# Dilated attention on one core: the high and low key halves of the strided branches as one moving operand, their logit halves added by VectorE

## The chip, the core and the metric

The kernel runs on one core of a Trainium2 chip. The metric is the device time of one launch in microseconds (us), from three timed runs and one profiled execution. TensorE ran at a granted clock of 0.999 of full speed over the profiled execution, which is the upper of its two levels, 2.4 GHz.

## What is computed

Two transformer blocks on 512 tokens of width 1024, all in float32. Only one stage of the second block is touched, the dilated attention: 8 heads of width 64, in three groups of keys (window 128 with dilation 1, window 512 with dilation 4, window 2048 with dilation 16), each with a bias per distance. The groups are merged by their row maxima and sums.

```python
s = jnp.einsum('bnqrhc,bnkrhc->bnrhqk', qb, kc) * (HEAD_DIM ** -0.5)
...
logits = jnp.where(valid[None, :, None, None], s + bias[None, None, None], NEG_INF)
m = jnp.max(logits, axis=-1)
p = jnp.exp(logits - m[..., None])
den = jnp.sum(p, axis=-1)
num = jnp.einsum('bnrhqk,bnkrhc->bnqrhc', p, vc)
```

## The kernel before

**Split operands.** TensorE multiplies in a rounded float32 format, so each operand is held as a high part (the rounded value) and a low part (the rest). A product is three matmuls into one PSUM sum: high times high, low times high, high times low. `mm3` (L514 to L518) does that for the dense layers, whose weights stream from memory in units of 128 x 1024: ScalarE rounds a unit (`whi`, L1125), VectorE makes the rest (`wlo`, L1421), TensorE multiplies it in 24 matmuls of 512 columns.

**The attention stage.** The 36 units of the query, key and value projection (`dil`) are multiplied one after the other. TensorE's stream is written by hand: after every second tile of a unit (6 matmuls) comes a "tick", and `attend(tick)` puts a piece of attention work there, by the tables `LOGITS_AT`, `TURN_AT`, `SUMS_AT`, `V_TURN_AT` and others. VectorE and ScalarE walk the same ticks in the same order. Attention is cut into 32 steps: four pairs of heads, each with four strided steps (`part` 0, the two dilated groups side by side, n = 0 to 3 of every eight) and four window steps (`part` 1). The two heads of a pair lie in partitions 0 to 63 and 64 to 127 of `dqk`, so that each logits matmul uses 64 rows. `dqk[rows, o, j, :]` holds for key group o the query high, query low, key high and key low (j = 0 to 3), 512 tokens each.

**One step n.** TensorE multiplies the logits (L972) into banks 2 and 3, one bank for each head. VectorE adds the bias into `dl` (L1957) and takes the negated row maxima (L1960). ScalarE takes the exponentials of both heads with their sums (L1388, `dp`). Two or three ticks after the logits TensorE transposes the probabilities (L984, "turned"), after a wait for the exponentials (`s_dac`). ScalarE and VectorE split them (L1378, L1944), and TensorE multiplies them with the values (L1001 and L1002, "sums"), after waits for the split probabilities and, in the first step of each branch, for the split values (`s_dvs`). The values are transposed by L1015 and split by VectorE (L1440 and L1441 into `dvt`). Before the logits of step n TensorE waits until VectorE has added the bias of step n - 1 (`s_dad`), because all steps use the same two banks.

**A strided step.** Keys are every fourth token: the moving operand is `dqk[r, o, b, t::4]`, 128 columns that lie 16 bytes apart. For each of two groups o and three products there is one matmul for each head, 12 in all.

In a strided step VectorE meets other duties in its fixed order: the projection rows that come out of the banks (L1887, L1470), the rest of the next weight unit (L1421), the value split (L1440, L1441), and the output addition (L1970).

Of the kernel before, what the change touches and what calls it, by code (L numbers as in the profile page):

```python
# [22 lines left out]
ALU = mybir.AluOpType  # L23
# [3 lines left out]
P = 128  # L27
T = 512
# [173 lines left out]
def build(nc, wst, xT, prm, cst, wup, wsT, bs, rb, onehot, fdram, out):  # L202
    es = ExitStack()
    with es:
        def sb(name, shape, dt=F32, st=es):
            return st.enter_context(nc.sbuf_tensor(name, shape, dt))

        def sem(name):
            return es.enter_context(nc.semaphore(name))
# [5 lines left out]
        h = sb("h", [P, KD, T])  # L215
# [18 lines left out]
        def bank(b, n=1):  # L234
            return PS[:, b * T:(b + n) * T]
# [58 lines left out]
        with ExitStack() as m:  # L294
# [3 lines left out]
            dqk = sb("dqk", [P, 3, 4, T], F32R, m)  # L298
# [4 lines left out]
            dl = sb("dl", [P, 2, 2, 256], F32, m)  # L303
# [48 lines left out]
        def bias_of(p):  # L352

            return (bias_a if p < 2 else bias_b)[:, 2 * (p % 2):2 * (p % 2) + 2, :]
# [139 lines left out]
        s_dtr = sem("dilated_transposed")  # L494
        s_dpv = sem("dilated_values_multiplied")
        s_dad = sem("dilated_bias_added")
        s_dlg = sem("dilated_logits_done")
        s_dco = sem("dilated_outputs_half_copied")
        s_dac = sem("dilated_exp_done")
# [14 lines left out]
        def mm3(pe, o, w, x, first, done, **kw):  # L514

            pe.matmul(o, w[0], x[0], start=first, stop=False, **kw)  # L516
            pe.matmul(o, w[1], x[0], start=False, stop=False, **kw)  # L517
            return pe.matmul(o, w[0], x[1], start=False, stop=done, **kw)  # L518
# [35 lines left out]
        def _(pe):  # L554
# [89 lines left out]
            for k, j in [(k, j) for k in range(KD) for j in range(2)]:  # L644
# [4 lines left out]
                ins = mm3(pe, bank(j), w_tile(j, k), x_tile(k), k == 0, k == KD - 1)  # L649
# [59 lines left out]
            for what, p in GLA_PLAN:  # L709
                if (what, p) in GLA_UNITS:  # L710
                    n = GLA_UNITS.index((what, p))
# [141 lines left out]
            for f in range(2):  # L853
                for j in range(4):
                    u = U0["cgv"] + 4 * f + j
                    unit_ready(u)
                    for kk in range(2):
                        k = 2 * j + kk
                        if f == 0:
                            pe.wait_ge(s_x, X0["ffout"] + k + 1)  # L860
                        for t in range(NT):
                            if f and k == 0 and t == 0:
                                pe.wait_ge(s_free, A0["cgu"])
                            if f and k == 0 and t >= 2:
                                pe.wait_ge(s_cac, t - 1)
                            c = slice(t * P, (t + 1) * P)
                            ins = mm3(pe, bank(CG_BANKS[f][t]), (xhi[:, k, c], xlo[:, k, c]),
                                      (whi[:, u % SLOTS, kk * T:(kk + 1) * T], wlo[:, u % SLOTS, kk * T:(kk + 1) * T]),
                                      k == 0, k == KD - 1)
# [7 lines left out]
            for n in range(2):  # L877
                ins = over_partitions(bank(4 + n), wsr[:, 0, 4 * n:4 * n + 4, :], wsr[:, 1, 4 * n:4 * n + 4, :])
# [77 lines left out]
            def logits(n):  # L956
                p, part, t = step_of(n)
                if n % 4 == 0:
                    pe.wait_ge(s_dqk, 6 * p + (6 if part else 4))
                if n:  # L960
                    pe.wait_ge(s_dad, n)
                rows = [slice(0, 64), slice(64, 128)]
                if part:
                    c = slice(T - (t + 1) * P, T - t * P)
                    k0 = (t - 1) * P if t else 0
                    blocks = [(2, c, slice(k0, (t + 1) * P), slice(0 if t else P, 2 * P))]
                else:
                    blocks = [(o, slice((3 - t) * P, (4 - t) * P), slice(t, T, 4), slice(o * P, (o + 1) * P)) for o in range(2)]
                for i, (o, q, k, c) in enumerate(blocks):
                    for a, b in ((0, 2), (1, 2), (0, 3)):  # L970
                        for x, r in enumerate(rows):
                            ins = pe.matmul(bank(2 + x)[:, c], dqk[r, o, a, q], dqk[r, o, b, k], start=i == 0 and (a, b) == (0, 2),  # L972
                                            stop=b == 3, skip_group_check=True)
                ins.then_inc(s_dlo, 1)
# [101 lines left out]
            for m in LAST_PARTS:  # L1076
                if m < 4:
                    acc_wait(A0["dilout"] + 4 + m)
                ins = mm3(pe, part_bank(m), w_tile(u % SLOTS, m), out_pair(3), m < 4, True)
# [332 lines left out]
        def _(dve):  # L1412
# [97 lines left out]
            for what, p in DVE_GLA_PLAN:  # L1510
                E = 11 * p
                if (what, p) in GLA_UNITS:
                    n = GLA_UNITS.index((what, p))
# [32 lines left out]
                elif what == "states":  # L1546

                    for x in range(2):
                        r = slice(64 * x, 64 * x + 64)
# [204 lines left out]
            for t in range(NT):  # L1754
                ins = dve.bn_aggr(mv[:, t, 0:2], st6[:, t, :, :].rearrange("p a b -> p (a b)"))
# [4 lines left out]
            for g in range(KD):  # L1760
                ins = dve.scalar_tensor_tensor(bsb[:, g, :], bank(4 + g // 4)[:, g % 4 * P:(g % 4 + 1) * P], par[:, C_LNB + g:C_LNB + g + 1],
                                               bsb[:, g, :], ALU.mult, ALU.add)
# [184 lines left out]
            def logits_masked(n):  # L1947

                p, part, t = step_of(n)
                o, tt = (oA, t) if part else (oB, 3 - t)  # L1950
                c0 = first_col(n)
                b0 = 0 if part else 256
                z = bank(2, 2).rearrange("p (x c) -> p x c", x=2)
                dve.wait_ge(s_dlo, n + 1)
                if n >= 2:
                    dve.wait_ge(s_dac, n - 1)
                dve.tensor_tensor(dl[:, n % 2, :, c0:], z[:, :, c0:256], bias_of(p)[:, :, b0 + c0:b0 + 256],  # L1957
                                  ALU.add).then_inc(s_dad, 1)
                dve.wait_ge(s_dad, n + 1)
                dve.tensor_reduce(o[:, tt, p, NMAX:ROW], dl[:, n % 2, :, c0:], AX, ALU.max, negate=True).then_inc(s_dlg, 1)  # L1960

# [27 lines left out]
            for tick in range(LAST_TICK):  # L1989
                k, q = tick // TICKS, tick % TICKS  # L1990
# [247 lines left out]
```

## Time and profile before

| | us |
|---|---|
| median of three runs | 1901.11 |
| lowest and highest | 1900.96, 1902.65 |
| the profiled execution, whole | 1901.1 |
| its span in the trace | 1899.4 |
| TensorE busy in the span | 1887.4 (99%) |
| VectorE busy | 1136.0 (60%) |
| ScalarE busy | 622.3 (33%) |

The profiled execution's time lies at the median of the runs; 1.7 us of it lie outside the traced span. The span is the time from the first to the last record. An engine's busy time is the union of its instructions. TensorE has two rows of records: PE for matmuls and PEld for the loads of the stationary operand, which run beside matmuls. The attention stage lies between 1276 and 1526 us of the span.

### The profile page before, as it was taken

To read this page: it belongs to the slowest core of one execution; us is meant where nothing else is said; L and a number is where in the kernel's file an instruction comes from. 1 tells how busy PE (TensorE), PEld (TensorE's weight loads), DVE (VectorE), ACT (ScalarE), POOL (GpSimd) and SP (SyncE) were. 2 spreads that over 40 slices of the span, in tenths; PEclk is the share of its full clock that TensorE was granted. 3 is DMA by queue.
4 is the path that set the end of the run, shared out by engine and by line. 5 is a ranking of instruction groups with operands and counts; after the bars stand their busy time and mean duration, and the time that the engine had idled before them with its cause. 6 is when DMAs were issued, how large, how long until landed. Compare 5 with 4: busy or idle time off the path is not lost.

```text
span 1899.4 us, 24463 instructions
## 1 busy us (share of the span) xinstructions
PE 1887.4 (99%) x9088; PEld 1560.0 (82%) x9088; DVE 1136.0 (60%) x1470; ACT 622.3 (33%) x846; POOL 140.9 (7%) x141
## 2 busy tenths in 40 slices
PE   9999999999999999999999999999999999999998
PEld 6888888888888888888888888888888888888887
DVE  7787777776666434675642354366766786325533
ACT  6313243343333233334322222323333353212221
POOL 0011002300000011002000000100110120000000
PEclk9999999999999999999999999999999999999999
DMA  4222222332233333222332443322222223332332
GB/s 166 67 78 90 78 67 78 100 100 93 95 99 99 96 114 124 79 85 84 111 95 95 116 119 99 98 89 73 79 72 73 62 69 121 100 100 89 99 100 67
DMA packets 54653, 176.48 MB, mean 93 GB/s; under 512 B 5875, under 2 KB 12291, under 8 KB 54572
## 3 DMA queue, kind: packets, MB, share of 16 engines
q1 hardware_dynamic: 49296, 170.82, 28.2%
q10 hardware_dynamic: 4764, 3.41, 0.8%
q0 software_dynamic: 512, 1.08, 0.2%
q8 instruction: 60, 0.98, 0.2%
q14 instruction: 21, 0.17, 0.0%
HBM read 172.09 MB, written 2.13 MB: 92 GB/s over the span
## 4 chain that ended last, share of the span: by engine, by line
PE 97%; DVE 2%; DMA 0%; issue 0%; ACT 0%; SPq 0%; DVEq 0%
PE ps L516 31%; PE ps L518 30%; PE ps L517 30%; PE ps L972 1%; PE ps L524 1%; PE ps L1001 1%; PE ps L984 1%; PE ps L1002 1%; PE ps L767 0%; DVE wlo L1421 0%; DVE yr L1440 0%; PE ps L1015 0%; DMA raw<-wst 0%; DVE h L2029 0%; DVE gate_a L1678 0%; DVE yr L1441 0%
## 5 line engine op out<-in xcount | busy, mean ns | idle before, releaser
L516 PE MATMUL ps<-xhi,whi 128*128 128x512 f32 x1576 | 624.4, 396 | 0.9 <-DVE xlo L1427 0.6
L518 PE MATMUL ps<-xlo,whi 128*128 128x512 f32 x1576 | 614.5, 390 | 0.0
L517 PE MATMUL ps<-xhi,wlo 128*128 128x512 f32 x1576 | 613.9, 390 | 0.0
L1421 DVE TENSOR_TENSOR wlo<-raw,whi 128x1024 fp32r<-128x1024 f32 x317 | 407.7, 1286 | 220.6 <-ACT whi L1125 220.3
L1125 ACT ACTIVATE whi<-raw 128x1024 fp32r<-128x1024 f32 x317 | 334.1, 1054 | 586.7 <-PE ps L518 530.9
L516 PEld LDWEIGHTS ps<-xhi,whi 128*128 128x128 f32 x1576 | 296.1, 188 | 67.4 <-DVE wlo L1421 3.7
L518 PEld LDWEIGHTS ps<-xlo,whi 128*128 128x128 f32 x1576 | 295.8, 188 | 63.1
L517 PEld LDWEIGHTS ps<-xhi,wlo 128*128 128x128 f32 x1576 | 296.2, 188 | 58.2 <-issue 0.2
L516 PE MATMUL ps<-mh,whi 128*128 128x512 f32 (+1 forms) x528 | 202.3, 383 | 0.0
L517 PE MATMUL ps<-mh,wlo 128*128 128x512 f32 (+1 forms) x528 | 202.0, 383 | 0.0
L518 PE MATMUL ps<-mh,whi 128*128 128x512 f32 (+1 forms) x528 | 202.0, 383 | 0.0
L516 PEld LDWEIGHTS ps<-mh,whi 128*128 128x128 f32 x528 | 99.2, 188 | 19.7 <-issue 0.4
L517 PEld LDWEIGHTS ps<-mh,wlo 128*128 128x128 f32 x528 | 99.3, 188 | 19.4
L518 PEld LDWEIGHTS ps<-mh,whi 128*128 128x128 f32 x528 | 99.3, 188 | 19.3
L1820 DVE SCALAR_TENSOR_TENSOR mr<-ps,rbc 128x512 f32<-128x512 f32 x64 | 44.1, 691 | 84.1 <-PE ps L518 84.0
L1456 DVE TENSOR_TENSOR h<-h,ps 128x512 f32 (+1 forms) x48 | 32.9, 686 | 101.4 <-PE ps L518 101.4
L1320 ACT ACTIVATE ms<-mr 128x512 f32<-128x512 f32 x48 | 30.3, 632 | 180.8 <-DVE mr L1820 180.8
L516 PE MATMUL ps<-hid,whi 128*128 128x512 f32 x176 | 68.5, 389 | 0.0
L517 PE MATMUL ps<-hid,wlo 128*128 128x512 f32 x176 | 68.5, 389 | 0.0
L518 PE MATMUL ps<-hid,whi 128*128 128x512 f32 x176 | 68.5, 389 | 0.0
L1427 DVE SCALAR_TENSOR_TENSOR xlo<-h,par,xhi 128x512 fp32r<-128x512 f32 (+1 forms) x48 | 39.5, 834 | 37.1 <-ACT xhi L1133 27.4
L2054 POOL TENSOR_TENSOR ssum<-ssum,sq 128x512 f32<-128x512 f32 x34 | 47.9, 1408 | 178.4 <-ACT sq L1137 178.1
(332 smaller groups left out, 2011.5 us busy)
## 6 DMA issues: line engine op xcount, KB each, us to landing
raw<-wst SPq DMA_DIRECT2D x317, 512.0 KB, 3.5
h<-xT SPq DMA_DIRECT2D x8, 256.0 KB, 5.9
out<-h SPq DMA_DIRECT2D x8, 256.0 KB, 2.3
oP<-oB POOLq DMA_DIRECT2D x16, 66.0 KB, 2.1
bias_a<-bias_rows ACTq DMA_DIRECT2D x4, 256.0 KB, 4.3
bias_b<-bias_rows ACTq DMA_DIRECT2D x4, 256.0 KB, 4.5
wsf<-wsT ACTq DMA_DIRECT2D x1, 512.0 KB, 3.4
bsb<-bs ACTq DMA_DIRECT2D x1, 512.0 KB, 4.3
```

The source lines that it names most:

```text
L516: pe.matmul(o, w[0], x[0], start=first, stop=False, **kw)
L517: pe.matmul(o, w[1], x[0], start=False, stop=False, **kw)
L518: return pe.matmul(o, w[0], x[1], start=False, stop=done, **kw)
L524: ins = pe.matmul(o, w[a], v[b], start=first and i == 0, stop=i == 2, skip_group_check=True)
L972: ins = pe.matmul(bank(2 + x)[:, c], dqk[r, o, a, q], dqk[r, o, b, k], start=i == 0 and (a, b) == (0, 2), stop=b == 3, skip_group_check=True)
L1125: act.activation(whi[:, n % SLOTS, :], raw[:, n % 2, :], ACT.Copy).then_inc(s_hi, 1)
L1320: act.activation(ms[:, m % 2, :], mr[:, m % 2, :], ACT.Square).then_inc(s_ms, 1)
L1421: dve.tensor_tensor(wlo[:, n % SLOTS, :], raw[:, n % 2, :], whi[:, n % SLOTS, :].bitcast(F32), ALU.subtract).then_inc(s_split, 1)
L1427: dve.scalar_tensor_tensor(xlo[:, m, :], h[:, m, :], gain, xhi[:, m, :].bitcast(F32), ALU.mult, ALU.subtract).then_inc(s_x, 1)
L1456: dve.tensor_tensor(hm, hm, bank(b), ALU.add).then_inc(s_free, 1)
L1820: dve.scalar_tensor_tensor(mr[:, m % 2, :], acc, 0.0, rbc[:, :], ALU.max, ALU.mult).then_inc(s_free, 1)
L2054: ins = pool.tensor_tensor(ssum[:, :], ssum[:, :], sq[:, n % 2, :], ALU.add)
```

## The change

In the strided steps the three matmuls of a head and a group become two. The first has the high query as stationary operand and, as one moving operand, the key high and key low together: `dqk[r, o, 2:4, k]`, 2 x 128 columns at the same distance of 16 bytes. It writes 256 columns of PSUM, high logits first and low logits behind them. The second, low query with high key, is added to the high logits. So a strided step has 8 matmuls, 4 of 256 columns and 4 of 128, and its logits take up 512 columns of a bank instead of 256. VectorE has one more operation in a strided step: the first adds the bias to the high logits into `dl`, and behind a new semaphore `s_dz` the second adds the low logits to that. Only the second lets TensorE go on in the banks. The window steps are as before.

```diff
+        s_dz = sem("dilated_high_logits_biased")
...
                 else:
-                    blocks = [(o, slice((3 - t) * P, (4 - t) * P), slice(t, T, 4), slice(o * P, (o + 1) * P)) for o in range(2)]
+                    for o in range(2):
+                        q, k = slice((3 - t) * P, (4 - t) * P), slice(t, T, 4)
+                        for x, r in enumerate(rows):
+                            pe.matmul(bank(2 + x)[:, 2 * o * P:2 * (o + 1) * P].rearrange("p (h c) -> p h c", h=2), dqk[r, o, 0, q],
+                                      dqk[r, o, 2:4, k], start=o == 0, stop=False, skip_group_check=True)
+                        for x, r in enumerate(rows):
+                            ins = pe.matmul(bank(2 + x)[:, 2 * o * P:(2 * o + 1) * P], dqk[r, o, 1, q], dqk[r, o, 2, k], start=False,
+                                            stop=True, skip_group_check=True)
+                    blocks = []
...
-                dve.tensor_tensor(dl[:, n % 2, :, c0:], z[:, :, c0:256], bias_of(p)[:, :, b0 + c0:b0 + 256],
-                                  ALU.add).then_inc(s_dad, 1)
+                if part:
+                    dve.tensor_tensor(dl[:, n % 2, :, c0:], z[:, :, c0:256], bias_of(p)[:, :, b0 + c0:b0 + 256],
+                                      ALU.add).then_inc(s_dad, 1)
+                else:
+                    zh = bank(2, 2).rearrange("p (x o h c) -> p x o h c", x=2, o=2, h=2)
+                    dve.tensor_tensor(dl[:, n % 2, :, :].rearrange("p x (o c) -> p x o c", o=2), zh[:, :, :, 0, :],
+                                      bias_of(p)[:, :, b0:b0 + 256].rearrange("p x (o c) -> p x o c", o=2), ALU.add).then_inc(s_dz, 1)
+                    dve.wait_ge(s_dz, 4 * p + n % 4 + 1)
+                    dve.tensor_tensor(dl[:, n % 2, :, :].rearrange("p x (o c) -> p (x o) c", o=2),
+                                      bank(2, 2).rearrange("p (y h c) -> p y h c", y=4, h=2)[:, :, 1, :],
+                                      dl[:, n % 2, :, :].rearrange("p x (o c) -> p (x o) c", o=2), ALU.add).then_inc(s_dad, 1)
```

On TensorE the logits of step 0 stand in one row before (`ps` is PSUM, `dqk` the queries and keys):

```order
4397 L972 MATMUL ps<-dqk 128x128 x12
```

and in four rows now:

```order
4397 L972 MATMUL ps<-dqk 128x256 x2
4398 L975 MATMUL ps<-dqk 128x128 x2
4399 L972 MATMUL ps<-dqk 128x256 x2
4400 L975 MATMUL ps<-dqk 128x128 x2
```

Nothing else on TensorE changes its place. On VectorE the stretch from the logits of step 0 to the value split behind step 1 is before (`dl` logits, `oB` row maxima, `dvf` the unturned values, `wlo` weights, `dpt` probabilities, `dvt` values):

```order
751 L1957 TENSOR_TENSOR dl<-ps,bias_a 128x512
752 L1960 TENSOR_REDUCE oB<-dl 128x2
753 L1470 TENSOR_TENSOR dvf<-ps,rbc 128x512
754 L1421 TENSOR_TENSOR wlo<-raw,whi 128x1024
755 L1944 TENSOR_TENSOR dpt<-ps,dpt 128x512
756 L1957 TENSOR_TENSOR dl<-ps,bias_a 128x512
757 L1960 TENSOR_REDUCE oB<-dl 128x2
758 L1440 CAST dvt<-ps 128x512
759 L1441 TENSOR_TENSOR dvt<-ps,dvt 128x512
```

and now (L1974 is the added operation, the other lines are the old ones under new numbers):

```order
751 L1971 TENSOR_TENSOR dl<-ps,bias_a 128x512
752 L1974 TENSOR_TENSOR dl<-ps,dl 128x512
753 L1978 TENSOR_REDUCE oB<-dl 128x2
754 L1479 TENSOR_TENSOR dvf<-ps,rbc 128x512
755 L1430 TENSOR_TENSOR wlo<-raw,whi 128x1024
756 L1953 TENSOR_TENSOR dpt<-ps,dpt 128x512
757 L1971 TENSOR_TENSOR dl<-ps,bias_a 128x512
758 L1974 TENSOR_TENSOR dl<-ps,dl 128x512
759 L1978 TENSOR_REDUCE oB<-dl 128x2
760 L1449 CAST dvt<-ps 128x512
761 L1450 TENSOR_TENSOR dvt<-ps,dvt 128x512
```

The row maxima and all behind them on VectorE stand one operation later, at each of the 16 strided steps.

## Rows read from the trace of the kernel before

**Rows 1.** The page, chain that ended last: shares of the span by engine

```profile
PE 97%; DVE 2%; DMA 0%; issue 0%; ACT 0%; SPq 0%; DVEq 0%
```

**Rows 2.** Windows view, the attention stage: length, busy time by engine, granted clock

```profile
1276.30:1526.00 249.70, 249.70 (x1459) 203.94 (x1459) 172.74 (x287) 90.26 (x228) 21.53 (x25) 1.00 0.22 69
```

**Rows 3.** Timeline, PE, strided step 0: start, duration, line, operands, count

```profile
1276.40 0.95 PE L972 MATMUL ps<-dqk 64*128 64x128 f32 x12
1277.28 0.50 PE L516 MATMUL ps<-xhi,whi 128*128 128x512 f32 x1
```

**Rows 4.** Timeline, PE, narrow windows inside step 0: the second and the fifth pair

```profile
1276.58 0.42 PE L972 MATMUL ps<-dqk 64*128 64x128 f32 x4
...
1276.94 0.41 PE L972 MATMUL ps<-dqk 64*128 64x128 f32 x4
```

**Rows 5.** Timeline, PE, window step 6: 256 columns without distance

```profile
1323.53 0.63 PE L972 MATMUL ps<-dqk 64*128 64x256 f32 x6
...
1323.75 0.40 PE L972 MATMUL ps<-dqk 64*128 64x256 f32 x4
...
1323.87 0.29 PE L972 MATMUL ps<-dqk 64*128 64x256 f32 x2
```

**Rows 6.** Source views, probability (L984) and value (L1015) transposes: ns, min/median/max

```profile
L984 PEld LDWEIGHTS ps<-con,dp x120: 137/140/143, 1280.0 to 1524.4; 128*128 128x128 f32 x120
L1015 PEld LDWEIGHTS ps<-con,dvf x48: 138/198/213, 1262.0 to 1512.4; 128*128 128x128 f32 x48
L1015 PE MATMUL ps<-con,dvf x48: 270/284/328, 1262.2 to 1512.5; 128*128 128x128 f32 x48
```

**Rows 7.** Timeline, PE: four value transposes read at every fourth token

```profile
1280.58 0.64 PE L1015 MATMUL ps<-con,dvf 128*128 128x128 f32 x4
```

**Rows 8.** Timeline, step 0 behind its logits: DVE, ACT, PE, PEld

```profile
1277.39 0.69 DVE L1957 TENSOR_TENSOR dl<-ps,bias_a 128x512 f32<-128x512 f32 x1 [3.31 <-PE ps L972]
1278.12 0.69 DVE L1960 TENSOR_REDUCE oB<-dl 128x2 f32<-128x512 f32 x1
...
1279.75 0.19 ACT L1388 ACTIVATION_READ_ACCUMULATOR dp<-dl,oB 128x1 f32 x1
...
1279.69 0.39 PE L517 MATMUL ps<-xhi,wlo 128*128 128x512 f32 x1
1279.91 0.40 PE L518 MATMUL ps<-xlo,whi 128*128 128x512 f32 x1
1280.15 0.27 PE L984 MATMUL ps<-con,dp 128*128 128x128 f32 x1
...
1279.99 0.30 PEld L984 LDWEIGHTS ps<-con,dp 128*128 128x128 f32 x2
```

**Rows 9.** Timeline, step 1 and the values that step 0 multiplies: DVE, PE

```profile
1283.55 0.69 DVE L1957 TENSOR_TENSOR dl<-ps,bias_a 128x512 f32<-128x512 f32 x1 [0.80 <-PE ps L972]
...
1285.59 0.69 DVE L1441 TENSOR_TENSOR dvt<-ps,dvt 128x512 fp32r<-128x512 f32 x1
...
1286.07 0.39 PE L518 MATMUL ps<-xlo,whi 128*128 128x512 f32 x1
1286.43 0.30 PE L1001 MATMUL ps<-dvt,dpt 128*128 128x128 f32 x1
```

**Rows 10.** Waits view, PEld, 1270 to 1530 us: total, times, longest

```profile
PEld ps L1001 <- issue: 1.3, 4, 0.4
```

**Rows 11.** Timeline, step 2: end of the exponentials (ACT), the transposes' loads (PEld)

```profile
1292.72 0.19 ACT L1388 ACTIVATION_READ_ACCUMULATOR dp<-dl,oB 128x1 f32 x1
...
1293.81 0.31 PEld L984 LDWEIGHTS ps<-con,dp 128*128 128x128 f32 x3
```

**Rows 12.** Timeline, step 28: bias addition (DVE), exponentials (ACT), transposes' loads (PEld)

```profile
1507.77 0.42 DVE L1957 TENSOR_TENSOR dl<-ps,bias_b 128x256 f32<-128x256 f32 x1 [0.20 <-PE ps L972]
...
1509.38 0.19 ACT L1388 ACTIVATION_READ_ACCUMULATOR dp<-dl,oA 128x1 f32 x1
...
1509.79 0.20 PEld L984 LDWEIGHTS ps<-con,dp 128*128 128x128 f32 x2
```

## The prediction

> **What bounds the kernel now.** I read the page first: TensorE is busy for 1887.4 of 1899.4 us (the table above), and the chain of waits runs through it for 97% [rows 1]. So a change counts by what it does to TensorE's own stream: work taken from it is gained in full, and a wait put into it is lost in full. The windows view of the attention stage says the same of that stretch: TensorE busy in all 249.7 us at full granted clock, VectorE in 172.7 [rows 2]. VectorE is no bound on average there. The question is whether TensorE waits for VectorE at single places, and for that I read timelines step by step: when VectorE or ScalarE finishes, when the waiting load starts on TensorE, and how much lies between.
>
> **What the strided logits cost TensorE.** In step 0 the 12 matmuls take from 1276.40 to the next dense matmul at 1277.28, 0.88 us [rows 3]. The two heads of a pair start together, so these are six pairs. The second starts at 1276.58 and the fifth at 1276.94 [rows 4]: one pair of 128 columns each 0.12 us. Two readings of that 0.12 us are possible, and the gain hangs on which is right.
>
> Reading one: a pair is held up by the load of its stationary operand, and the columns are hidden behind it. For it speaks window step 6, where a pair has 256 columns side by side and the next starts after 0.12 us too, 1323.75 to 1323.87 [rows 5]: twice the columns for the same time. Then four pairs instead of six save 2 x 0.12 = 0.24 us, less some 0.04 us since the first pair of 256 columns holds the second up for 0.22 us (1323.53 to 1323.75) [rows 5] where one of 128 does for 0.18 (1276.40 to 1276.58) [rows 3, 4]. That is 0.20 us for each step, 16 x 0.20 = 3.2 us in all.
>
> Reading two: reading columns that lie 16 bytes apart is slow in itself, and it holds the pair up. The value transposes show what such a distance costs on the stationary side: mostly read at every fourth token, they load in 198 ns (median, up to 213; the least, 138, are those of the group without a distance) where the probabilities' transposes load in 137 to 143 ns [rows 6]. Four of them, read at a distance, take 0.64 us [rows 7]; less 0.28 us for the last one itself (the median of their matmuls [rows 6]) and over three intervals that is 0.12 us from one to the next. So 128 columns read at a distance take 0.12 us there, the same as a pair's 0.12 us in the logits. By this reading the moving operand passes 128 columns each 0.12 us, and the change saves nothing: each head reads 6 x 128 = 768 columns before and 2 x 256 + 2 x 128 = 768 after. Only the number of instructions falls.
>
> The Trainium skill ("Advanced Engine Details and Errata", Memory Cachelines) says that SBUF has lines of 16 bytes and that reads which each meet another line are slower. Four float32 values are 16 bytes, so each column here meets another line; the skill gives no figure for it. That rule speaks for reading two, and the trace's longer loads agree.
>
> I take reading two, since two different operands show the same 0.12 us, and since the window step's 256 columns have no distance and so say nothing about a read with one. The saving is 0 us, the bound from below; the bound from above is 3.2 us.
>
> **What VectorE's added operation costs.** It has the shape of the operation beside it, which takes 0.69 us and lets the next one that depends on it start 0.73 us after its own start (1277.39 to 1278.12) [rows 8]. So in each of 16 steps the row maxima, the exponentials and the transposes' data come 0.73 us later, 16 x 0.73 = 11.7 us of VectorE. In 249.7 us with 77 idle [rows 2] there is room for that on average. Where TensorE has no cover it waits:
>
> *Transposes of the first strided step of each pair (steps 0, 8, 16, 24).* In step 0 ScalarE ends at 1279.75 + 0.19 = 1279.94, the load of the transposes starts at 1279.99, 0.05 us behind it, and their first matmul follows the dense one by 0.24 us (1279.91 to 1280.15), where dense matmuls follow each other by 0.22 to 0.23 (1279.69 to 1279.91) [rows 8]. The load is released just in time: no wait is seen, and none of the 0.73 us has cover. Steps 8, 16 and 24 repeat the pattern with the same 0.05 us. 4 x 0.73 = 2.9 us.
>
> *Values for the same four steps.* Step 0 multiplies with values that VectorE splits behind the row maxima of step 1. The second half of the split ends at 1285.59 + 0.69 = 1286.28; the matmul with the values starts at 1286.43, 0.36 us behind the dense one at 1286.07 [rows 9]. TensorE waits here already, by 0.36 - 0.23 = 0.13 us. The waits view has four such waits and no fifth [rows 10]. VectorE had idled for 0.80 us before the logits of step 1 came [rows 9], so the whole row from the bias addition to the split hangs on these logits, and the added operation moves the split by 0.73 us. 4 x 0.73 = 2.9 us.
>
> *Transposes of the other twelve strided steps.* They stand behind the previous step's value matmuls and have cover. The least is in step 2: ScalarE ends at 1292.72 + 0.19 = 1292.91, the load starts at 1293.81 [rows 11], 0.90 us. From this go 0.73 us, and VectorE, which has one more operation in front of this step's logits too, may meet them later than now. Between nothing and 0.3 us; I take 0.1.
>
> *Behind the last strided step.* Before step 28's addition at 1507.77 VectorE has 0.20 us idle [rows 12], and nearly none between step 27's addition and that. So step 28's addition starts 0.73 - 0.20 = 0.53 us later. Its exponentials end at 1509.38 + 0.19 = 1509.57 and then at 1510.10, but the transposes' load stands at 1509.79 [rows 12]. With 0.05 us to release it, TensorE waits for 0.3 to 0.45 us; I take 0.4.
>
> *The banks.* Before the next logits TensorE waits for the second addition now. It ends some 1.5 us behind the logits, and steps 0 and 1 have their additions 6.2 us apart (1277.39 to 1283.55) [rows 8, 9]: cover of over 3 us, no cost, and the other strided steps lie about as far apart. If VectorE fell so far behind, this would be the first new wait of logits. Weight units and projection rows stand behind the added operation in VectorE's order too; a unit is needed three units later and a bank one unit later, several us each, so they cost nothing.
>
> **Sum.** Saved 0. Added 2.9 + 2.9 + 0.1 + 0.4 = 6.3 us. The profiled execution took 1901.1 us, 1.7 of it outside the span, and the median is 1901.11, so the same base serves for both: 1901.1 + 6.3 = 1907.4 us.
>
> **The rivals.**
>
> *A. The columns are hidden (reading one).* The saving is up to 3.2 us, the waits stay: with shorter logits VectorE's duties of step 2 come closer together, so some 6.5 us. 1901.1 + 6.5 - 3.2 = 1904.4; with a read that is only half as slow, 1905.5. For it: the window step's pairs. Against it: the loads with a distance. A change of 0.2% (3.8 us) is about what a measurement of this kernel can tell from none, and this case lies across that line.
>
> *B. Faster: hidden columns, and no place without cover.* The saving of 3.2 us stays and VectorE's second addition is covered everywhere: if the load at 1279.99 was late for a reason of its own and not by ScalarE's end, and the value split could go ahead of the row. 1901.1 - 3.2 = 1897.9. It decides from the point where the eight tight places together cost under 3.2 us, 0.4 each instead of 0.73; to be faster by over 0.2% they must cost nothing. Against it: 0.05 us between ScalarE's end and the load, four times alike [rows 8], and the four waits that are there already [rows 10].
>
> *C. VectorE falls behind.* If the additions take longer than 0.69 us on logits in pieces of 128 columns (0.1 us more is 8 x 0.1 = 0.8 us at the tight places), or the covers of 0.90 us and more in the other steps do not hold, 2 to 3 us come on top: about 1910. Against it: VectorE has idle time before the logits of most steps, which takes a delay up.
>
> **How the numbers follow.** The forecast has a chance of 0.62, A 0.23, B 0.04, C 0.11. The forecast by itself reaches from 1906.4 to 1908.4, by the terms of step 2 and step 28 and 0.05 us at each of eight places. With A the range goes down to 1904.0, with C up to 1909.8; what lies outside is B and the edges of A and C. Slower by over 0.2% (above 1904.9) takes the forecast, C, and some of A: 0.82. Within 0.2% takes the rest of A and a little of B: 0.14. Faster is what is left of B: 0.04.
>
> **What would show it.** In the profile of the changed kernel: the logits of a strided step take 0.88 us from their start to the next dense matmul, and the matmul behind a 256-column pair starts 0.24 us after it; at 0.68 us and 0.12 us rival A holds. The first transposes of steps 0, 8, 16 and 24 follow the dense matmul by about 0.96 us, and the first value matmuls of the same steps by about 1.09 us, where it was 0.24 and 0.36. The row from VectorE's first addition to the row maxima takes 1.45 us instead of 0.73. The strided steps 1 to 3 of each pair show almost no new wait. The forecast is wrong if the eight places show waits of less than 0.4 us, or if other places wait as well.

## The result, and the profile after

| | before | after |
|---|---|---|
| median, us | 1901.11 | 1908.49 (7 runs, 1907.27 to 1909.11) |
| ratio after to before | | 1.0033, interval 1.0023 to 1.0043 |
| the profiled execution, whole | 1901.1 | 1907.3 |
| its span | 1899.4 | 1905.2 |
| first logits of the stage start at | 1276.40 | 1276.16 |
| between the same two dense matmuls | 257.88 | 263.41 |

The change makes the kernel slower by 0.33%. The last row of the table is the measure that the rest of this text goes by: the time from a dense matmul ahead of the attention stage (it starts at 1272.23 us before, at 1271.99 after) to one behind it (1530.11 and 1535.40). The same matmuls are counted off in every kernel. It is needed because the timed runs of each kernel fall at two levels some 1.5 us apart (before: most at 1900.9 to 1901.1 or at 1902.2 to 1902.8; after: 1907.3 to 1907.6 or 1908.5 to 1909.1), with the median of before in its lower and that of after in its upper, and level against level the change costs 6.3 to 6.4 us. In the traces the difference lies ahead of the stage and goes with TensorE's clock: from 20 to 40 us the granted clock is 1.00 before and after and 0.91 in the trace of e1, an experiment below, whose stage starts 1.6 us later than that of before. The stage has grown by 5.53 us, the span by 5.8.

The page of the kernel after, busy times and shares of the chain that ended last:

```profile
PE 1888.5 (99%) x9024; PEld 1558.1 (82%) x9024; DVE 1146.2 (60%) x1486; ACT 622.0 (33%) x846; POOL 140.8 (7%) x141
...
PE 96%; DVE 3%; issue 0%; ACT 0%; DMA 0%; DVEq 0%; ACTq 0%
```

64 matmuls are gone (16 steps of four), and TensorE is busy 1.1 us longer, not shorter. VectorE has 10.2 us more. In the chain a per cent has gone from TensorE to VectorE, against [rows 1]. Read alone, this page would not show what happened: no engine is nearer its limit than it was.

The strided logits of step 0, against [rows 3, 4]:

```profile
1276.16 0.48 PE L972 MATMUL ps<-dqk 64*128 64x256 f32 x2
1276.46 0.30 PE L975 MATMUL ps<-dqk 64*128 64x128 f32 x2
1276.58 0.41 PE L972 MATMUL ps<-dqk 64*128 64x256 f32 x2
1276.81 0.30 PE L975 MATMUL ps<-dqk 64*128 64x128 f32 x2
1277.04 0.50 PE L517 MATMUL ps<-xhi,whi 128*128 128x512 f32 x1
```

From 1276.16 to 1277.04 are 0.88 us, as before. The pair of 128 columns at 1276.46 is followed after 0.12 us, the pair of 256 at 1276.58 after 0.23 us. Twice the columns take twice the time. (The first pair, at 1276.16, is followed after 0.30 us.)

Step 0 behind its logits (VectorE, ScalarE, TensorE, then its load), against [rows 8]:

```profile
1277.15 0.69 DVE L1971 TENSOR_TENSOR dl<-ps,bias_a 128x512 f32<-128x512 f32 x1 [3.31 <-PE ps L975]
1277.88 0.69 DVE L1974 TENSOR_TENSOR dl<-ps,dl 128x512 f32<-128x512 f32 x1
1278.60 0.69 DVE L1978 TENSOR_REDUCE oB<-dl 128x2 f32<-128x512 f32 x1
...
1280.23 0.19 ACT L1397 ACTIVATION_READ_ACCUMULATOR dp<-dl,oB 128x1 f32 x1
...
1279.66 0.39 PE L519 MATMUL ps<-xlo,whi 128*128 128x512 f32 x1
1280.47 0.66 PE L993 MATMUL ps<-con,dp 128*128 128x128 f32 x4 [0.42 <-ACT dp L1397]
...
1280.47 0.14 PEld L993 LDWEIGHTS ps<-con,dp 128*128 128x128 f32 x1 [0.84 <-ACT dp L1397]
```

From the first addition to the row maxima it is 1.45 us where it was 0.73. ScalarE ends at 1280.42, and TensorE, which issued its last dense matmul at 1279.66, goes on at 1280.47: 0.81 us between the two, where it was 0.24.

Step 1, and the values that step 0 multiplies, against [rows 9]:

```profile
1283.92 0.69 DVE L1971 TENSOR_TENSOR dl<-ps,bias_a 128x512 f32<-128x512 f32 x1 [0.70 <-PE ps L975]
...
1286.69 0.69 DVE L1450 TENSOR_TENSOR dvt<-ps,dvt 128x512 fp32r<-128x512 f32 x1
...
1286.44 0.39 PE L519 MATMUL ps<-xlo,whi 128*128 128x512 f32 x1
1287.53 0.30 PE L1010 MATMUL ps<-dvt,dpt 128*128 128x128 f32 x1 [0.70 <-DVE dvt L1450]
```

The split ends at 1287.38, and the value matmul starts at 1287.53, 1.09 us behind the dense one at 1286.44. It was 0.36.

The waits of TensorE's loads in the stage, against [rows 10] (total, times, longest):

```profile
PEld ps L1010 <- issue: 4.3, 4, 1.1
...
PEld ps L993 <- ACT dp L1397: 3.7, 5, 0.8
```

L1010 is the value matmul (L1001 before): four waits as before, 4.3 us instead of 1.3. L993 is the probabilities' transpose (L984): five waits where the kernel before has none in this view. Four of them are steps 0, 8, 16 and 24, the fifth is step 28:

```profile
1513.23 0.41 DVE L1967 TENSOR_TENSOR dl<-ps,bias_b 128x256 f32<-128x256 f32 x1
...
1514.83 0.19 ACT L1397 ACTIVATION_READ_ACCUMULATOR dp<-dl,oA 128x1 f32 x1
...
1515.07 0.44 PE L993 MATMUL ps<-con,dp 128*128 128x128 f32 x2 [0.19 <-ACT dp L1397]
```

VectorE no longer idles ahead of step 28's addition, where [rows 12] has 0.20 us.

**Where the 5.53 us lie.** Intervals between the starts of neighbouring matmuls, summed by kind over the stage, after less before:

| interval | us |
|---|---|
| dense to transposes, steps 0, 8, 16, 24 (0.23 to 0.81 each) | +2.30 |
| inside the groups of transposes | +0.23 |
| dense to values, the same steps (0.31 to 0.35, now 1.05 to 1.09) | +2.95 |
| logits to transposes, step 28 (0.20 to 0.46) | +0.26 |
| inside the logits and behind them, 16 steps | -0.09 |
| between dense matmuls, and all others | -0.12 |
| sum | +5.53 |

### The profile page after: what moved, and what is told of

Its sections match the earlier page's. It is cut to its first block, busy times and chain, and to the rows that moved or that the text cites. A ratio compares the mean times of both kernels' runs of the same rounds, so it can differ in the third digit from the quotient of the medians.

```text
span 1905.2 us, 24351 instructions
## 1 busy us (share of the span) xinstructions
PE 1888.5 (99%) x9024; PEld 1558.1 (82%) x9024; DVE 1146.2 (60%) x1486; ACT 622.0 (33%) x846; POOL 140.8 (7%) x141
## 4 chain that ended last, share of the span: by engine, by line
PE 96%; DVE 3%; issue 0%; ACT 0%; DMA 0%; DVEq 0%; ACTq 0%
PE ps L517 30%; PE ps L519 30%; PE ps L518 30%; PE ps L525 1%; PE ps L1010 1%; PE ps L993 1%; PE ps L972 1%; DVE wlo L1430 1%; PE ps L1011 1%; PE ps L768 0%; PE ps L981 0%; DVE yr L1449 0%; PE ps L1024 0%; DVE h L2047 0%; DVE gate_a L1687 0%
```

## Experiments

"Stage" is the time between the two dense matmuls, given as the difference to the kernel before (257.88 us). Each experiment was timed in five rounds beside the kernel before, whose medians there were 1902.54 us (e1 to e4), 1902.22 (e5 to e8, on another chip) and 1902.49 (e9 to e12).

| kernel | stage, us | ratio to before | interval |
|---|---|---|---|
| after | +5.53 | 1.0033 | 1.0023 to 1.0043 |
| e1 TensorE's part alone | -0.15 | 0.9995 | 0.9986 to 1.0004 |
| e2 VectorE's part alone | +5.69 | 1.0036 | 1.0022 to 1.0049 |
| e3 only steps 2 and 3 of each pair | +0.23 | 1.0001 | 0.9992 to 1.0010 |
| e4 only steps 0 and 1 | +5.34 | 1.0028 | 1.0017 to 1.0038 |
| e5 after, keys gathered | +1.29 | 1.0012 | 1.0003 to 1.0021 |
| e6 before, keys gathered | -1.33 | 0.9997 | 0.9988 to 1.0007 |
| e7 after, values split earlier | +3.19 | 1.0019 | 1.0010 to 1.0028 |
| e8 after, transposes later | +5.89 | 1.0040 | 1.0027 to 1.0054 |
| e9 after, logits earlier | +3.01 | 1.0015 | 1.0006 to 1.0024 |
| e10 after, e7 and e9 together | -0.63 | 0.9999 | 0.9990 to 1.0008 |
| e11 e5 with e7 and e9 | -4.15 | 0.9980 | 0.9971 to 0.9989 |
| e12 e6 with e7 and e9 | -2.11 | 0.9990 | 0.9981 to 0.9999 |

The theory: the merged matmuls save nothing, since the distance of the columns sets their pace, and all of the loss is VectorE's added operation at nine places without cover. The rivals: the columns are hidden and the saving is eaten by something else (A), or VectorE falls behind everywhere (C).

### e1 and e2: each half of the change alone

Against the kernel after, e1 keeps TensorE's 8 matmuls for each strided step, and VectorE adds the high half only. The low keys are multiplied, and their part of the logits is left out.

```diff
-                                      bias_of(p)..., ALU.add).then_inc(s_dz, 1)
-                    dve.wait_ge(s_dz, 4 * p + n % 4 + 1)
-                    dve.tensor_tensor(dl[...], bank(2, 2)...[:, :, 1, :], dl[...], ALU.add).then_inc(s_dad, 1)
+                                      bias_of(p)..., ALU.add).then_inc(s_dad, 1)
```

> The changed kernel's eight matmuls in the strided steps, but VectorE adds only the bias to the high half of the logits; the half with the low keys is multiplied and left out of the sum. My theory (a read at a distance of 16 bytes sets the pace, the time is lost by VectorE's later row maxima): the logits of a strided step still take 0.88 us, none of the eight tight places waits for more than before, and the time is that of the kernel before, 1901 us, within 1 us. Rival A (columns hidden, four pairs cost less than six): 0.68 us a step and 3.2 us less than before, 1898 us. Third theory, that the wider logits themselves (512 columns of each bank) delay somebody: still 4 us or more above the kernel before.

e2 has 12 matmuls of 128 columns again, which write the layout of the kernel after, and keeps VectorE's two additions.

```diff
-                        for x, r in enumerate(rows):
-                            pe.matmul(bank(2 + x)[...].rearrange("p (h c) -> p h c", h=2), dqk[r, o, 0, q], dqk[r, o, 2:4, k], ...)
+                        for h in range(2):
+                            for x, r in enumerate(rows):
+                                pe.matmul(bank(2 + x)[:, (2 * o + h) * P:(2 * o + h + 1) * P], dqk[r, o, 0, q], dqk[r, o, 2 + h, k], ...)
```

> The reverse: twelve matmuls of 128 columns as before, but high keys and low keys into separate columns of the bank as in the change, and VectorE adds the halves with the second operation. My theory: the same waits as in the changed kernel, 0.57 us at the first transposes and 0.73 us at the value matmuls of steps 0, 8, 16, 24, and the same time as the changed kernel within 1 us (6 to 7 us above the kernel before). Rival A: 3 us slower than the changed kernel.

Measured: e1 -0.15 us in the stage and no difference in the timed runs, e2 +5.69 us. Step 0 of e1 on TensorE, its logits and then its transposes:

```profile
1278.03 0.48 PE L972 MATMUL ps<-dqk 64*128 64x256 f32 x2
1278.32 0.30 PE L975 MATMUL ps<-dqk 64*128 64x128 f32 x2
1278.44 0.41 PE L972 MATMUL ps<-dqk 64*128 64x256 f32 x2
1278.67 0.30 PE L975 MATMUL ps<-dqk 64*128 64x128 f32 x2
1278.90 0.50 PE L517 MATMUL ps<-xhi,whi 128*128 128x512 f32 x1
...
1281.53 0.39 PE L519 MATMUL ps<-xlo,whi 128*128 128x512 f32 x1
1281.76 0.60 PE L993 MATMUL ps<-con,dp 128*128 128x128 f32 x4
```

0.87 us for the logits with eight matmuls and nothing else changed, and the transposes follow after 0.23 us. The same of e2:

```profile
1276.44 0.48 PE L973 MATMUL ps<-dqk 64*128 64x128 f32 x4
...
1277.32 0.50 PE L517 MATMUL ps<-xhi,whi 128*128 128x512 f32 x1
...
1279.95 0.39 PE L519 MATMUL ps<-xlo,whi 128*128 128x512 f32 x1
1280.76 0.65 PE L994 MATMUL ps<-con,dp 128*128 128x128 f32 x4 [0.41 <-ACT dp L1398]
1281.25 0.65 PE L1025 MATMUL ps<-con,dvf 128*128 128x128 f32 x4
```

0.88 us for the logits, 0.81 from the dense matmul to the transposes. So the whole loss is VectorE's half, and TensorE's half is worth a tenth of a microsecond. That tells the forecast from rival A: by A, e1 would have come out up to 3.2 us faster. It doesn't yet say why the merged matmuls save nothing; e5 does.

### e3 and e4: where the added operation costs

e3 makes the change only in steps 2 and 3 of each pair of heads, e4 only in steps 0 and 1; the others are as before. The edit of e3 to the kernel after (e4 has `t < 2` for `t >= 2`; in both, the count that VectorE waits for at `s_dz` is changed to two steps for each pair):

```diff
+                elif not (t >= 2):
+                    blocks = [(o, slice((3 - t) * P, (4 - t) * P), slice(t, T, 4), slice(o * P, (o + 1) * P)) for o in range(2)]
...
-                if part:
+                if part or not (t >= 2):
```

> The change in the strided steps 2 and 3 of each pair only; steps 0 and 1 as before. My theory: eight added operations of 0.73 us on VectorE, all of them under cover but for the last one before step 28, so 0 to 0.5 us above the kernel before. Rival (the added operations cost VectorE's time wherever they stand, 16 of them some 6.4 us): half of it, 3.2 us above.

> The change in the strided steps 0 and 1 of each pair only, the two whose row maxima stand before a tight place: step 0 before its own transposes, step 1 before the value split. My theory: nearly the whole loss of the change, 4 x (0.57 + 0.73) = 5.2 us in the trace and 5 to 7 us in the timed runs. Rival (as above): half, 3.2 us.

Measured: +0.23 and +5.34 us, together 5.57 where the whole change has 5.53. In e3 the waits view has one entry for the transposes' load, that of step 28, and the values' four waits are as in [rows 10]:

```profile
PEld ps L1012 <- issue: 1.3, 4, 0.4
PEld ps L995 <- ACT dp L1399: 0.4, 1, 0.4
```

Eight added operations, 5.8 us of VectorE, cost 0.2 us; the other eight cost 5.3. That speaks against rival C: were it VectorE's load as such, both halves would cost about the same.

### e5 and e6: why the merged matmuls save nothing

In e5 the kernel after gets its keys laid out residue by residue, as the queries are already, so that the 128 keys of a step lie side by side. e6 does the same to the kernel before. The edits are two, where the keys leave the bank and where the logits read them:

```diff
-                if j == 0 and o < 2:
-                    back = dst.rearrange("p (r q) -> p q r", r=4)[:, ::-1, ::-1]
+                if o < 2:
+                    back = dst.rearrange("p (r q) -> p q r", r=4)
+                    if j == 0:
+                        back = back[:, ::-1, ::-1]
...
-    slice(t, T, 4)
+    slice(t * P, (t + 1) * P)
```

> The changed kernel with the strided groups' keys laid out residue by residue in dqk, as the queries are already, so that the moving operand's 128 columns lie side by side. My theory (the distance of 16 bytes sets the pace of the logits): the logits of a strided step fall from 0.88 to about 0.67 us, the first 256-column pair is followed after 0.22 us and the second after 0.12 instead of 0.29 and 0.23; the waits of VectorE's second addition stay at 0.57 and 0.73 us. About 3.2 us under the changed kernel, 3 us above the kernel before. Rival (256 columns out of two places of dqk are slow by themselves, not by their distance): no difference from the changed kernel.

> The kernel before (twelve matmuls, one addition) with the same gathered keys. My theory: a pair goes from 0.118 to 0.109 us, the logits of a strided step from 0.88 to 0.82 us, 1.0 us under the kernel before in all: too little for the timed runs to tell, to be read in the trace. If a distance costs what half of the column pace costs, a pair would go to 0.06 us and the step to 0.5 us: this I don't expect, since the load of the stationary operand then sets the pace at 0.11 us.

Measured: e5 needs 0.60 us for the logits of a step, where after has 0.88. Step 0 of e5:

```profile
1277.88 0.39 PE L972 MATMUL ps<-dqk 64*128 64x256 f32 x2
1278.10 0.22 PE L975 MATMUL ps<-dqk 64*128 64x128 f32 x2
1278.16 0.33 PE L972 MATMUL ps<-dqk 64*128 64x256 f32 x2
1278.33 0.22 PE L975 MATMUL ps<-dqk 64*128 64x128 f32 x2
1278.48 0.50 PE L517 MATMUL ps<-xhi,whi 128*128 128x512 f32 x1
```

The instructions are those of after, only the distance of the columns has gone. A pair of 128 columns is followed after 0.06 us (1278.10 to 1278.16) instead of 0.12, and its record lasts 0.22 us instead of 0.30. So the distance set the pace, and with it the 768 columns of each head took the same time in eight matmuls as in twelve. The Trainium skill ("Advanced Engine Details and Errata", Memory Cachelines) says of reads that meet another 16-byte line each time: "performance penalty"; the trace agrees, and puts it at about twice the time for a column.

Step 0 of e6, twelve matmuls on gathered keys:

```profile
1277.87 0.89 PE L972 MATMUL ps<-dqk 64*128 64x128 f32 x12
1278.68 0.50 PE L516 MATMUL ps<-xhi,whi 128*128 128x512 f32 x1
```

0.81 us, only 0.07 less than before, though the columns themselves need half the time. The intervals between pairs are 0.11 us, and the loads' records start 0.11 us apart too, as they do in the kernel before. I take it that here the load holds the pair up; that it is not the columns e5 shows, but no run separates the load from any other cost of one more instruction. So both readings of the prediction are true, each of its own case. At a distance the columns set 0.12 us for each 128, gathered the loads set 0.11 us for each pair, and the two lie so near each other that the kernel before could not tell them apart. The merge pays only where the load is the limit: from e6 to e5 a step's logits go from 0.81 to 0.60 us.

Over the whole kernel e5 is 0.12% slower than before. It gains 16 x 0.28 = 4.5 us in the logits and loses 5.9 us to the waits of after and to one more: with the logits shorter, the transposes of step 2 come 0.26 us behind the values, where it was 0.08.

### e7, e8 and e9: three ways to cover the tight places

e7 moves VectorE's value split of the second group ahead of the additions of step 1, in the kernel after. `values_split(v)` holds the lines that stood under `if tick in V_SPLIT_AT`; between the two pieces stand the additions and row maxima of the tick.

```diff
+                if tick in V_SPLIT_AT and V_SPLIT_AT[tick] % 3 == 1:
+                    values_split(V_SPLIT_AT[tick])
...
-                if tick in V_SPLIT_AT:
+                if tick in V_SPLIT_AT and V_SPLIT_AT[tick] % 3 != 1:
```

> The changed kernel, but at the tick of step 1 VectorE splits the turned values before it adds the logits of step 1, so that the split no longer hangs on the added operation. My theory: the four value matmuls' waits go (1.06 to 1.09 us back to 0.23), and the transposes of step 1, whose cover is 0.5 us now and loses some 0.6 to the split, wait for 0.1 to 0.4 us instead. 1.5 to 3 us under the changed kernel. Rival (the value matmuls wait for something else, such as the split probabilities): no difference.

Measured: +3.19 us. The values' waits are gone, and new ones have come. VectorE and ScalarE in step 1 of e7, then TensorE:

```profile
1284.01 0.69 DVE L1450 TENSOR_TENSOR dvt<-ps,dvt 128x512 fp32r<-128x512 f32 x1
1284.61 0.68 DVE L1971 TENSOR_TENSOR dl<-ps,bias_a 128x512 f32<-128x512 f32 x1
...
1287.69 0.19 ACT L1397 ACTIVATION_READ_ACCUMULATOR dp<-dl,oB 128x1 f32 x1
...
1286.59 0.39 PE L519 MATMUL ps<-xlo,whi 128*128 128x512 f32 x1
1286.82 0.22 PE L1010 MATMUL ps<-dvt,dpt 128*128 128x128 f32 x1
...
1287.55 0.24 PE L1011 MATMUL ps<-dvt,dpt 128*128 128x64 f32 x1
1287.93 0.66 PE L993 MATMUL ps<-con,dp 128*128 128x128 f32 x4
```

The value matmul follows the dense one after 0.23 us. But the additions of step 1 now start 0.65 us behind their logits, the exponentials end at 1287.88, and the transposes of step 1 start 0.38 us behind the last value matmul, where it was 0.08. Four such places and step 2 take 1.4 us of the 3.6 that the values give back.

e8 puts TensorE's transposes of steps 0, 8, 16 and 24 one tick later, e9 puts their logits one tick earlier. e8:

```diff
-        LOGITS_AT[_d + 3 * _s], TURN_AT[_d + 3 * _s + 2], SUMS_AT[_d + 3 * _s + 5] = _n, _n, _n
+        LOGITS_AT[_d + 3 * _s], TURN_AT[_d + 3 * _s + (2 if _s else 3)], SUMS_AT[_d + 3 * _s + 5] = _n, _n, _n
```

and e9:

```diff
-        LOGITS_AT[_d + 3 * _s], TURN_AT[_d + 3 * _s + 2], SUMS_AT[_d + 3 * _s + 5] = _n, _n, _n
+        LOGITS_AT[_d + 3 * _s - (0 if _s else 1)], TURN_AT[_d + 3 * _s + 2], SUMS_AT[_d + 3 * _s + 5] = _n, _n, _n
```

> The changed kernel, but the transposes of the first strided step of each pair stand one tick later (6 dense matmuls, 1.4 us). The waits of 0.57 us at these transposes go. If the two tight places add up, 4 x 0.57 = 2.3 us under the changed kernel. If one takes over from the other (the later transposes keep VectorE waiting for their split in its order, and the value split of step 1 comes later against TensorE), the value matmuls wait for more than 1.06 us and the time stays within 1 us of the changed kernel; I hold the second for more likely (0.6).

> The changed kernel with the logits of the first strided step of each pair one tick (6 dense matmuls, 1.4 us) earlier; its transposes stay where they are. That gives cover to the chain without putting its transposes behind anybody in VectorE's order. If the transposes' wait is a term of its own: 0.57 us back to none at four places, the value matmuls still at 1.06, 4 x 0.57 = 2.3 us shorter than the changed kernel in the attention stage (256.6 to 254.3 us). If it only passes to the value matmuls, as with the transposes one tick later: their gap grows to about 1.6 us and nothing is gained.

Measured: e8 +5.89 us, no gain at all; e9 +3.01 us, 2.5 us given back. In both the transposes follow the dense matmul after 0.23 us. In e8 the wait has only moved on. VectorE, then TensorE:

```profile
1285.10 0.69 DVE L1971 TENSOR_TENSOR dl<-ps,bias_a 128x512 f32<-128x512 f32 x1 [0.81 <-PE ps L975]
...
1287.15 0.68 DVE L1953 TENSOR_TENSOR dpt<-ps,dpt 128x512 fp32r<-128x512 f32 x1
...
1288.47 0.69 DVE L1450 TENSOR_TENSOR dvt<-ps,dvt 128x512 fp32r<-128x512 f32 x1
...
1287.61 0.39 PE L519 MATMUL ps<-xlo,whi 128*128 128x512 f32 x1
...
1289.30 0.30 PE L1010 MATMUL ps<-dvt,dpt 128*128 128x128 f32 x1 [1.31 <-DVE dvt L1450]
```

The split of the probabilities (L1953) stands behind step 1's additions now, between them and the value split, which therefore ends 0.60 us later still. The value matmul starts 1.69 us behind the last dense one, where after has 1.09. These 4 x 0.60 us eat up the 2.5 us that the transposes give back, and another 0.5 us lies among the matmuls that changed places. In e9 the values keep their 1.04 to 1.09 us, and only the transposes' wait goes: what starts the row earlier helps, what consumes it later moved other work into the row.

### e10, e11 and e12: all covers, and the kernel that beats both

e10 is the kernel after with the edits of e7 and e9. e11 is e5 with both, e12 is e6 with both.

> The changed kernel with both: logits of steps 0, 8, 16, 24 one tick earlier, and the value split ahead of the logits of step 1. Both kinds of tight place covered: if VectorE's added operation costs only there, the stage is back to that of the kernel before, 251.1 us, but for 0.26 us behind step 28 and some 0.3 to 0.6 us where steps 1 and 2 lose cover; within 1 us of the kernel before in the timed runs. If the added operations cost something else too, 2 us or more stay.

> The same two covers with the keys gathered (eight matmuls that take 0.60 us a step instead of 0.88, two additions). The candidate for a version faster than both: the gathered kernel's stage of 252.4 us less 4 x 0.59 for the transposes and some 1 to 2 us for the values, 248 to 249.5 us, 2 to 3 us under the kernel before. If VectorE's dense stretch behind step 1 now takes the cover away (the logits come sooner), 250 us or more.

> The kernel before (twelve matmuls, one addition) with gathered keys and the same two covers. 16 x 0.067 = 1.1 us from the gathered keys and 4 x 0.13 = 0.5 us from the value matmuls' wait that was there already: 249.4 us, 1.7 us under the kernel before. The run beside the one with eight matmuls tells whether the halves' addition is worth its place once the keys are gathered: with eight matmuls 0.21 us a step less on TensorE, 3.4 us, against what waits are left there.

Measured: e10 -0.63 us. All eight places follow after 0.23 us, and of the transposes' five waits one is left, that of step 28:

```profile
PEld ps L993 <- ACT dp L1397: 0.4, 1, 0.4
```

VectorE works as much as in after (busy for 1146.8 us), 16 additions more than before, and the time is that of the kernel before: 0.9999. So the 16 additions cost almost nothing once the places have cover. The 0.63 us is no gain of the change either: e10 has also lost the waits of the values that the kernel before has, 0.7 us with what they cost inside the groups. With the keys still at a distance, there is nothing to win by the change even then.

e11 is the fastest kernel of this study: -4.15 us in the stage, 1898.64 against 1902.49 us in the same rounds, 0.20% faster than before with an interval of 0.9971 to 0.9989. Its waits for the exponentials:

```profile
PEld ps L993 <- ACT dp L1397: 1.2, 5, 0.4
```

The logits give back 4.5 us. Of the waits, five are left or new: steps 9, 17 and 25 and step 2, whose transposes come 0.31 to 0.40 us behind the values instead of 0.08, and step 28. e12 has -2.11 us and a ratio of 0.9990. So of e11's gain half needs neither the merge nor VectorE's second addition, and the merge itself is worth 2.0 us, once the keys are gathered and the places covered. Without the covers the merge on gathered keys costs 2.6 us (e5 against e6).

## Why the prediction was right

Predicted were 1907.4 us in a range from 1904.0 to 1909.8, and 0.82 for slower by over 0.2%. Measured were 1907.3 us for the profiled execution, against whose counterpart the sum was made, and a median of 1908.49. The mechanism was right, what sets the pace of the logits and where TensorE waits. That the total comes so close, 6.2 us measured for 6.3, is partly luck: see the sum below.

**What the strided logits cost.** The choice of reading two held. "The matmul behind a 256-column pair starts 0.24 us after it": 0.23. The logits take 0.88 us. The saving is 0.1 us, not 0, and e5 shows the mechanism. What the prediction didn't see is that reading one is true as well, 0.01 us below: it took the window step's 0.12 us as saying nothing about the case. It says what gathered keys would give. The choice itself rested on thinner ground than it looked. Of "two different operands show the same 0.12 us", the transposes are a weak half: those of the probabilities, without any distance, follow each other by 0.109 us in the kernel before, against 0.120 for the values'. The longer loads, 198 against 140 ns, were the better sign.

**Transposes of the first strided step of each pair.** The place was right, "none of the 0.73 us has cover" was not. Predicted 4 x 0.73 = 2.9 us and a first matmul 0.96 us behind the dense one; measured 0.81 us, 2.3 us in all. Before, the load starts at 1279.99 and the matmul at 1280.15, 0.16 us later [rows 8]; after, both records start at 1280.47. Against the dense matmul ahead of it, the load did come 0.73 us later. The 0.16 us between load and matmul, which lay beside the last dense matmul before, was the cover that the prediction left out. A little of it is lost again inside the group: with load and matmul starting together, the four transposes take 0.06 us more (1280.76 to 1281.25 is 0.49 us in e2), 0.23 us for the four groups. The term is 2.5 us where 2.9 was said.

**Values for the same four steps.** Predicted 2.9 us, measured 2.95, and 1.09 us in step 0 as said. Here TensorE waited before already, so nothing was left to cover the delay, and the whole of it went through.

**The other twelve, and behind the last.** Predicted 0.1, measured nothing: no wait in steps 1 to 3 of any pair, which e3 confirms. Step 28: predicted 0.4, measured 0.26 us. The addition of step 28 starts 0.56 us behind its logits instead of 0.11, 0.45 us later, not 0.53.

**The sum.** Predicted 6.3, measured 5.5 in the stage and 5.8 over the span. Of the difference 0.4 is the transposes' term, 0.24 the two small ones, 0.1 each the logits and the dense matmuls. What filled the gap to the 6.2 us of the whole execution is in no term of the prediction. Behind the stage are 0.50 us, all of them in the last four transposes of the program, which follow the same matmuls as before and run at the lower level of the clock, 1.2 GHz, in this trace. Windows view, before and after (the stretch, its length, busy times by engine; the last three numbers are granted clock, DMA share, GB/s):

```profile
1892.75:1893.46 0.71, 0.71 (x4) 0.52 (x4) 0.00 (x0) 0.00 (x0) 0.00 (x0) 1.00 0.92 316
...
1898.03:1899.25 1.22, 1.22 (x4) 0.93 (x4) 0.00 (x0) 0.00 (x0) 0.00 (x0) 0.50 0.64 215
```

Of the experiments' traces only that of e9 has the same; e2 has both additions everywhere and ends as the kernel before does. So nothing ties these 0.50 us to the change. Ahead of the stage the trace of after is 0.24 us shorter. And outside the span lie 2.07 us where the sum took the old 1.7: every run of a kernel with all 16 added operations has 2.05 to 2.21 us there (after, e2, e5, e7 to e11), every run of one with eight or none 1.68 to 1.80. That is a cost of the change of some 0.36 us which was put at nothing; why it arises stays open.

**The rivals.** A fell with e1. Its mechanism is real with gathered keys, at the price that it was given: 0.20 us for each step, and from e6 to e5 it is 0.81 less 0.60 us. B, that the places have cover after all, fell with the trace of after; e10 shows what cover would have taken, and that even then its other half, the hidden columns, is missing. C fell with the rows of after, where both additions take 0.69 us and the transposes of steps 1 to 3 of a pair show no new wait, and with e3.

## What to carry to other kernels

Before instructions are merged, ask what sets their pace: if two causes give the same number (here 0.12 us by the columns' distance, 0.11 by the load), find a row in which one of them is absent. An operation added on an engine that is 60% busy costs nearly its full time at every place where its result is consumed just in time (here 0.63 and 0.73 of 0.73 us), and almost nothing elsewhere; count those places rather than the engine's idle time (here 8 of the 16 added operations carry 5.3 of the 5.5 us). Of the cover, count the consumer's own lead too, down to the load that runs ahead of its matmul, and when a place is covered look which duty has slipped into the row behind it.

## What the runs showed of the hardware

- Moving columns at a distance of 16 bytes, float32, 64 rows, two heads side by side: 0.12 us for 128 columns and 0.23 for 256. Side by side: 0.06 for 128 behind a pair of 256 (e5).
- Gathered pairs of 256 and 128 columns in turn: the four intervals of a step are 0.22, 0.06, 0.17 and 0.15 us (e5), 0.60 in all, where 0.67 had been expected from the intervals of other steps. With twelve matmuls of 128 columns a pair takes a steady 0.11 us (e6). In e5 the loads of the four pairs start at 1277.88, 1277.98, 1278.10 and 1278.21, so they keep an even pace beside the uneven matmuls. What makes the short interval possible was not tried.
- How far a load runs ahead of its matmul depends on what stands before it. Behind a dense matmul without a wait it is 0.16 to 0.23 us for the first transpose and 0.22 for the first value matmul; behind value matmuls, and for a transpose whose load had to wait, both records start together (1280.47 for both). A value matmul whose load had to wait starts 0.03 us behind it.
- A group whose first load has no lead takes longer inside: 0.38 us from the first to the fourth transpose instead of 0.33, and 0.805 us from the first to the eighth value matmul instead of 0.73 (the 0.30 us that e7 gains inside its value groups, over four steps). The transposes behind value matmuls show the same 0.38 us without any wait.
- The same four transposes of 128 columns take 0.71 us at a granted clock of 1.00 (before) and 1.22 us at 0.50 (after).
